# Six weight places, in-place low parts, late factors for two feed-forward norms, and grouped 512-column matmuls in a three-layer float32 forward pass

## The reference

```python
for l in range(2):                                   # first kind
    h = rmsnorm(x, g_mix[l]);  proj = h @ w_in[l]    # gates, convolution, three attentions
    branch = einsum('bsnc,ncd->bsnd', ys, w_branch[l])
    x = x + sum(sigmoid(gate) * branch) @ w_out[l]
    x = x + conv_ffn(rmsnorm(x, g_ffn[l]), w_up[l], ..., w_down[l])     # D_FF = 2816
h = rmsnorm(x, norm_mix_2);  ...                     # second kind: SSD, LRU, retention
x = x + merged @ w_o_2
x = x + conv_ffn_2(rmsnorm(x, norm_ffn_2), ...)      # FFN_DIM = 3072
out = rmsnorm(x, norm_final_2)

def rmsnorm(x, g): return x * rsqrt(mean(x * x, -1) + EPS) * g
def conv_ffn(h, w_up, conv_w, conv_b, w_down):
    gate, up = split(depthwise_conv(h @ w_up, conv_w, conv_b))
    return (silu(gate) * up) @ w_down
```

## Time and profile before

| | |
|---|---|
| three runs | 1458.43, 1458.99, 1459.16 us |
| profiled execution | 1458.09 us, of it 1456.3 us span of the core |
| TensorE busy | 1435.8 us, 99% of the span |
| GpSimd busy | 1183.8 us, 81% |
| ScalarE busy | 886.1 us, 61% |
| VectorE busy | 660.0 us, 45% |
| chain that ended last | 93% on TensorE, 2% VectorE, 2% ScalarE, 1% issue, 1% DMA |
| read from HBM | 249.56 MB, 172 GB/s over the span |

### The profile page before, as it was taken

The page is one execution under the profiler, slowest core; times in us unless marked ns, Lnnn a source line. Parts: engine busy times, 40 slices in busy tenths (PEclk is TensorE's granted clock), DMA queues, the critical chain, the costliest instruction groups (busy, mean ns, idle before and its releaser), DMA issues.

```text
span 1456.3 us, 29049 instructions
## 1 busy us (share of the span) xinstructions
PE 1435.8 (99%) x9420; PEld 1294.2 (89%) x9420; DVE 660.0 (45%) x1478; ACT 886.1 (61%) x1496; POOL 1183.8 (81%) x926
## 2 busy tenths in 40 slices
PE   8999999999999999999999999999999999999998
PEld 7899998888888899988888889999899999888887
DVE  3653444444445733355444456660563642433333
ACT  5665645766666655647666666866445544655554
POOL 5876686999879876787998979899576899789895
PEclk9999999999999999999999999999999999999999
DMA  7654454666556544454665666556444565566663
GB/s 246 201 159 146 145 160 144 199 193 187 188 178 202 167 153 143 150 178 144 198 190 189 184 212 199 161 176 188 130 145 125 152 189 185 157 190 186 190 188 101
DMA packets 80036, 251.80 MB, mean 173 GB/s; under 512 B 7632, under 2 KB 22480, under 8 KB 79440
## 3 DMA queue, kind: packets, MB, share of 16 engines
q1 hardware_dynamic: 79088, 245.72, 54.3%
q10 hardware_dynamic: 864, 4.92, 0.9%
HBM read 249.56 MB, written 1.05 MB: 172 GB/s over the span
## 4 chain that ended last, share of the span: by engine, by line
PE 93%; DVE 2%; ACT 2%; issue 1%; DMA 1%; POOL 0%; SPq 0%; DVEq 0%; ACTq 0%; POOLq 0%
PE psum L922 20%; PE psum L923 20%; PE psum L924 20%; PE psum L956 18%; PE psum L957 9%; PE psum L1033 1%; PE psum L1021 1%; DMA raw<-in_units 1%; PE psum L1052 1%; PE psum L1043 1%; DVE x L1463 1%; ACT w_hi L428 0%; PE psum L1316 0%; PE psum L1111 0%; PE psum L1352 0%
## 5 line engine op out<-in xcount | busy, mean ns | idle before, releaser
L403 POOL TENSOR_TENSOR w_lo<-raw,w_hi 128x512 fp32r<-128x512 f32 x461 | 602.8, 1308 | 257.2 <-ACT w_hi L428 247.6
L404 POOL TENSOR_TENSOR w_lo<-raw,w_hi 128x512 fp32r<-128x512 f32 x461 | 609.1, 1321 | 0.0
L428 ACT ACTIVATE w_hi<-raw 128x1024 fp32r<-128x1024 f32 x461 | 484.7, 1054 | 92.3 <-PE psum L924 76.6
L956 PE MATMUL psum<-both,w_hi 128*128 128x512 f32 x1088 | 387.6, 399 | 0.0
L922 PE MATMUL psum<-both,w_hi 128*128 128x256 f32 x1192 | 345.4, 290 | 2.3 <-POOL w_lo L404 2.3
L924 PE MATMUL psum<-both,w_hi 128*128 128x256 f32 x1192 | 336.9, 283 | 0.0
L923 PE MATMUL psum<-both,w_lo 128*128 128x256 f32 x1192 | 336.9, 283 | 0.0
L957 PE MATMUL psum<-both,w_lo 128*128 128x256 f32 x1088 | 305.3, 281 | 0.0
L956 PEld LDWEIGHTS psum<-both,w_hi 128*128 128x128 f32 x1088 | 204.3, 188 | 51.2 <-POOL w_lo L404 0.4
L922 PEld LDWEIGHTS psum<-both,w_hi 128*128 128x128 f32 x1192 | 228.0, 191 | 11.8 <-issue 8.6
L923 PEld LDWEIGHTS psum<-both,w_lo 128*128 128x128 f32 x1192 | 228.2, 191 | 0.3
(11 more groups left out here) (276 smaller groups left out, 2118.6 us busy)
## 6 DMA issues: line engine op xcount, KB each, us to landing
raw<-in_units SPq DMA_DIRECT2D x461, 512.0 KB, 3.6
arena<-in_consts ACTq DMA_DIRECT2D x1, 2320.0 KB, 9.4
arena<-in_bias ACTq DMA_DIRECT2D x2, 1024.0 KB, 5.0
arena<-in_consts SPq DMA_DIRECT2D x1, 1657.0 KB, 8.4
out<-arena SPq DMA_DIRECT2D x4, 256.0 KB, 2.6
pre<-in_x SPq DMA_DIRECT2D x2, 256.0 KB, 2.9
arena<-in_x SPq DMA_DIRECT2D x2, 256.0 KB, 4.7
prm<-in_params ACTq DMA_DIRECT2D x2, 153.5 KB, 3.4
```

What stands on the lines that cost most here:

```text
L403: pool.tensor_tensor(w_lo[s][:, 0:D // 2], raw[s][:, 0:D // 2], w_hi[s][:, 0:D // 2].bitcast(F32), ALU.subtract)
L404: pool.tensor_tensor(w_lo[s][:, D // 2:D], raw[s][:, D // 2:D], w_hi[s][:, D // 2:D].bitcast(F32), ALU.subtract)\
L428: act.activation(w_hi[s][:, :], raw[s][:, :], ACT.Copy).then_inc(hi_ready, d.inc(hi_ready))
L956: pe.matmul(bank(4 + k), blocks_of(w_hi[s], c), both[:, 2 * c * T:2 * (c + 1) * T], start=(c == 0), stop=False, skip_group_check=True)
```

## The change

It has these parts:

1. There are six places for weights. `w_lo[s]` lies in the same memory as `raw[s]`, so the low part is written over the raw weights. SyncE now waits for TensorE to be done with unit u-6 before it loads unit u. ScalarE's `high()` waits only for the landing, and GpSimd only for the high part. Six units are loaded at the start.
2. ScalarE makes one high part more ahead at the start (`norm(..., 4)` for 3). In the feed-forward norms two `high()` stand where one stood, and the one after the first two feed-forwards is gone.
3. The norms ahead of the three feed-forwards are late: `late_norm`. x is turned unscaled, by transposes, between the pieces of the last product (`last_two_turning`). h's parts are made of x times g. The factor of each token is made meanwhile, spread over the partitions by two small matmuls into bank 2, and copied to `rstd`. `add_low` multiplies each up unit's sum by it, one more VectorE instruction for each of the 136 up units.
4. The first two up units run together, chunk by chunk. Every other up unit has its eight 512-column matmuls first and then its eight of 256 columns.
5. Five loops of TensorE and ScalarE in the third layer are written out.

```diff
 RING = 4
+W_RING = 6
...
-        raw = [sb(f"raw{s}", D) for s in range(RING)]
-        w_hi = [sb(f"w_hi{s}", D, F32R) for s in range(RING)]
-        w_lo = [sb(f"w_lo{s}", D, F32R) for s in range(RING)]
+        raw = []
+        with ExitStack() as landing:
+            for s in range(W_RING):
+                raw.append(landing.enter_context(nc.sbuf_tensor(f"raw{s}", [P, D], F32)))
+        w_lo = [sb(f"w_lo{s}", D, F32R) for s in range(W_RING)]
+        w_hi = [sb(f"w_hi{s}", D, F32R) for s in range(W_RING)]
...
+            d.skip(unit_done, RING)
+            def landing_free(u):
+                if u is None or u >= W_RING:
+                    sp.wait_ge(unit_done, d.next(unit_done))
...
-            def load(index, s):
-                sp.wait_ge(hi_ready, d.next(hi_ready))
-                sp.wait_ge(lo_ready, d.next(lo_ready))
+            def load(index, s, u=None):
+                landing_free(u)
...
             def low(s):
-                pool.wait_ge(raw_full[s], d.next(raw_full[s]))
                 pool.wait_ge(hi_ready, d.next(hi_ready))
-                pool.wait_ge(unit_done, d.next(unit_done, 1, "slot"))
...
                     act.wait_ge(raw_full[s], d.next(raw_full[s]))
-                    act.wait_ge(unit_done, d.next(unit_done, 1, "slot"))
                     act.activation(w_hi[s][:, :], raw[s][:, :], ACT.Copy).then_inc(hi_ready, d.inc(hi_ready))
...
+            def late_norm(gain, spare):
+                act.activation(small[:, 57:58], small[:, 60:61], ACT.Sqrt)
+                act.wait_ge(x_ready, d.next(x_ready, 2))
+                act.activation(tok(arena, 2), tok(x, 0), ACT.Square, accum_out=small[:, 0:1])
+                act.wait_ge(x_ready, d.next(x_ready))
+                act.activation(tok(arena, 3, 0, 512), tok(x, 1, 0, 512), ACT.Square, accum_out=small[:, 1:2])\
+                    .then_inc(part_ready, d.inc(part_ready))
+                for c in range(CH):
+                    if c % 4 == 0:
+                        act.wait_ge(turned, d.next(turned))
+                    if c >= 2:
+                        act.wait_ge(hlo_ready, d.next(hlo_ready))
+                    act.activation(chunk(h_hi, c), raw_chunk(c, spare), ACT.Copy, scale=prm[:, gain + c:gain + c + 1])\
+                        .then_inc(hhi_ready, d.inc(hhi_ready))
+                    if c == 3:
+                        high()
+                ...
+                high()
+                act.wait_ge(factors, d.next(factors))
+                act.activation(rstd[:, :], bank(2, 0, T), ACT.Copy).then_inc(rows_ready, d.inc(rows_ready))
...
-                norm(load_params1, P1["g_mix"], 2 if layer else 3, True)
+                norm(load_params1, P1["g_mix"], 2 if layer else 4, True)
...
-                norm(lambda: None, P1["g_ffn"], 1)
+                late_norm(P1["g_ffn"], SPARE1)
...
                         feed_high(jj % 2, jj % 2 * 2 + 1)
-                high()
...
                 for c in range(CH):
-                    if first is not None:
-                        pe.wait_ge(first, d.next(first))
                     pe.matmul(bank(4 + k), blocks_of(w_hi[s], c), both[:, 2 * c * T:2 * (c + 1) * T], start=(c == 0), stop=False, skip_group_check=True)
+                for c in range(CH):
                     last = pe.matmul(slot(k), blocks_of(w_lo[s], c), chunk(h_hi, c), start=False, stop=(c == CH - 1), skip_group_check=True)
...
+            def last_two_turning(hi, lo, c, ready):
+                ...
+                for half, g in ((0, 0), (0, 1), (1, 0)):
+                    for k in range(2):
+                        ...
+                        last = piece(half, g, k)
+                    last.then_inc(acc_done, d.inc(acc_done))
+                pe.wait_ge(slot_free, d.value(slot_free, "wait", -RING))
+                pe.wait_ge(x_ready, d.next(x_ready, 2))
+                turn_raw(0, range(CH))
+                piece(1, 1, 0).then_inc(unit_done, d.inc(unit_done))
+                pe.wait_ge(x_ready, d.next(x_ready))
+                turn_raw(1, range(4)).then_inc(turned, d.inc(turned))
+                piece(1, 1, 1).then_inc(unit_done, d.inc(unit_done))
...
             def feed_forward(n):
-                up_unit(hlo_ready)
-                for _ in range(3):
+                pair = []
+                for _ in range(2):
+                    pair.append((unit(), next_slot()))
+                    pe.wait_ge(slot_free, d.next(slot_free))
+                for c in range(CH):
+                    pe.wait_ge(hlo_ready, d.next(hlo_ready))
+                    for s, k in pair:
+                        ...
+                    if c == 1:
+                        pe.wait_ge(x_ready, d.next(x_ready))
+                        turn_raw(1, range(4, CH)).then_inc(turned, d.inc(turned))
+                pe.wait_ge(root_rows, d.next(root_rows))
+                for half in range(2):
+                    last = pe.matmul(bank(2, half * P, P), small[:, 4 + half:5 + half].to_broadcast([P, P]), ident, start=True, stop=True)
+                last.then_inc(factors, d.inc(factors))
+                for _ in range(2):
                     up_unit()
...
-                last_two(y_hi, y_lo, 2 * CH - 2, flo_ready)
-                turn_norm()
+                last_two_turning(y_hi, y_lo, 2 * CH - 2, flo_ready)
...
                 dve.wait_ge(low_out, d.next(low_out))
-                dve.tensor_tensor(slot(k), slot(k), low_part(k)[1], ALU.add).then_inc(sum_ready, d.inc(sum_ready))
+                dve.tensor_tensor(slot(k), slot(k), low_part(k)[1], ALU.add).then_inc(vec, d.inc(vec))
+                dve.wait_ge(d.last, d.made(d.last))
+                dve.tensor_tensor(slot(k), slot(k), rstd[:, :], ALU.mult).then_inc(sum_ready, d.inc(sum_ready))
...
+            def late_norm(gain, spare):
+                ...
+                for q in range(3):
+                    dve.wait_ge(acc_done, d.next(acc_done))
+                    add(q)
+                dve.wait_ge(part_ready, d.next(part_ready))
+                dve.tensor_scalar(small[:, 3:4], small[:, 1:2], 1.0 / D, EPS, ALU.mult, ALU.add).then_inc(rest_ready, d.inc(rest_ready))
+                h_low(0)
+                dve.wait_ge(unit_done, d.next(unit_done))
+                add(3)
+                for c in range(1, CH):
+                    h_low(c)
+                d.skip(turned, 2)
+                dve.wait_ge(sd_ready, d.next(sd_ready))
+                dve.reciprocal(small[:, 4:6], small[:, 6:8]).then_inc(root_rows, d.inc(root_rows))
+                dve.wait_ge(rows_ready, d.next(rows_ready))
```

144 lines of the change are left out of this document (83 added, 61 removed).

## The result

The changed kernel took 1479.03 us (median of 4 runs, 1476.20 to 1482.27), the kernel before on the same chip 1459.08 us (1458.43 to 1459.23). The ratio is 1.0138, with a 95% interval of 1.0126 to 1.015: slower by 20 us. The forecast was 1463.2 us, with a range that ended at 1467.5.

What follows compares the result with a forecast made beforehand. TensorE, busy 1435.8 of 1456.3 us at full clock, was taken as the bound. 2 x 2.1 + 2 x 2.1 + 0.8 + 0.5 - 5.5 = +4.2 us gave 1462.3, as a median 1463.2; range 1455.3 to 1467.5.

Steps and rivals of the forecast that it cites:

- At the start: Start of the program: six early loads and wider prefetch change nothing TensorE waits for; 0, within 0.5 us either way.
- The boundary: Step from the last product into the feed-forward: the fifth up unit starts 2.1 us later in each of the first two.
- the third boundary: Same step into the third feed-forward: one scaled copy, then the Gelu waits for two taps; unit 393 0.8 us later.
- The ends: Ends of the feed-forwards: late copy and multiply add 2.1 us in each of the first two, 0.5 in the third.
- The grouping: Up units' matmuls ordered by size, 118 units counted: 5.5 us saved.
- The rival that it gives nothing: Up units: the order of sizes may not cause the slow pace, so no saving; +9.7 us, 1468.7; chance 12%.
- The steady loop: Feed-forward loops: ScalarE is held back but with room; the 136 multiplies, 58 us, lie in VectorE's idle time.
- the fourth rival: GpSimd becomes the bound because each multiply holds it up: 1470 to 1480 us; chance 4%.
- The third rival: Attention and third layer: `high()` waits for fresh landings, making ScalarE late; +3 us more, 1466; chance 12%.
- The first: Boundaries and ends: weights land before ScalarE comes to the `high()`, leaving only the multiply; 3.5 us less, 1455.5; chance 20%.

Runs made afterwards that it cites:

- e2: The changed kernel, with SyncE issuing units 4 and 5 and the table of constants only when the first norm's parameters have landed: 1475.67 us, ratio 1.011.
- e9: The changed kernel, with only the table of constants held back until the first parameters have landed: 1474.09 us, ratio 1.0107.
- e5: The changed kernel plus 15 useless 512-column matmuls behind the fourth up unit of each feed-forward, filling TensorE's wait: 1469.32 us, ratio 1.0067.
- e3: The changed kernel, with both copies of low sums ahead of the high part at the first tile of the first two feed-forwards: 1469.41 us, ratio 1.0072.
- e4: The changed kernel, with ScalarE one high part less ahead through the feed-forwards: 1461.83 us, ratio 1.0022.
- e8: The changed kernel with e2's edit, first-tile copies ahead of the high part in all feed-forwards, and one high part less ahead in the first two: 1452.46 us.
- e6: The changed kernel without the multiply of each up unit's sum by the token's factor: 1475.49 us, ratio 1.0112.
- e1: The kernel before with only the matmuls grouped by size, in up units outside the first of each feed-forward: 1453.55 us, ratio 0.9963.
- e7: The changed kernel with the feed-forward norms of before, no multiply, ScalarE's old order around them, and e2's edit: 1454.79 us, ratio 0.9971.
- e10: The kernel of e8 run again, beside e11 on one chip: 1452.48 us, ratio 0.9954.
- e11: The kernel before with the grouped matmuls alone, run again beside e10 on one chip: 1454.43 us, ratio 0.9967.

## Why the prediction was wrong

The side was right, the size was not: +4.2 us forecast, +18 in the trace and +20 in the median. Two things were priced at nothing and one term was too small.

**The failed steps.** *"At the start ... the six early loads and the wider prefetch change nothing that TensorE waits for: 0, within 0.5 either way."* It was +4.54 us, 3.88 of it from the late parameters. I weighed what the loads do to GpSimd's pace and not what else was in flight. The parameters' DMA at 10.6 us was in the trace of before, with 3.2 us to landing, and the order of SyncE's queue was in the diff. e2 shows the cause, e9 that it was the table and not the two units. The other 0.66, at unit 4, came from a late high part.

*The price of a wait.* Each wait that I added was priced at its length. The earlier trace rows show a full clock in every slice, and I took that as given instead of as something that TensorE's steady work keeps up. The waits that I forecast myself, near 4 us at unit 72 and near 2.7 at the ends, let it fall at three of the four places where the wait was about 3.5 us, 7.2 us in all. e5 shows this by filling the wait, e3 by taking it away. With both mistakes off (4.5 + 7.2 = 11.7) the trace would be 6.4 us longer than before, against 4.2.

**The boundary** was right in mechanism and size. Without the clock the steps are 3.46 - 1.57 = 1.9 and 4.66 - 2.84 = 1.8 us against 2.1; the wait was 3.57 for 3.9, and the third boundary +0.86 for +0.8. e3 and e4 show both parts of it, the high part between the copies and the landing.

**The ends** had the right mechanism; the term was too small: 2.9, and 5.85 - 2.81 = 3.0, for 2.1. I had the copy late by 1.8 and it was late by 2.5: unit 129 ended at 426.67 and the weights that take its place were there at 430.99, 4.3 us later, where I had counted 3.7. Why this landing took longer than the median is open. The multiply's share, 0.47 in e4 and e8, was as worked out (0.5) where no landing is in the way.

**The grouping** gave 1.59 + 1.60 + 1.74 = 4.9 us for 5.5, and 5.3 alone. The rival that it gives nothing is out. The Trainium skill's page "TensorE: Matmul & The Clock Gate" (LDWEIGHTS, step by step) says only that the next weights load while a matmul runs; what fails for this stream is the step from there to "the order of the sizes doesn't matter".

**The steady loop** was right: ScalarE waits for landings everywhere, and TensorE for nothing. Nearly all of the 136 multiplies are hidden. GpSimd's halves take 1306 and 1316 ns in the changed kernel, 1308 and 1316 without the multiply (e6) and 1308 and 1321 before, so neither the multiplies nor the six places slow it, which was the fourth rival. The third rival, late high parts in the attentions, was worth 0.4 us and not 3, with 0.66 more at unit 4. The first, loads in time, failed on the landing: ScalarE came to unit 74's `high()` 1.31 us ahead of it.

## What to carry to other kernels

Price a wait of a busy TensorE at its length, and one of some 2 us or more at 1.5 to 2.8 us on top in case the clock falls; a single stop may cost more than a hundred hidden instructions. When loads are brought forward, list every other transfer that is issued after them and ask who waits for it first. A ring with more places moves the wait from "the place is free" to "the transfer has landed"; look for the one instruction behind such a wait that others need, and put it ahead.

## What the runs showed of the hardware that was not expected

- The clock's fall is not certain. Over the thirteen traces, behind the first 12 us, among TensorE's waits of 2 us and more, it did not fall behind 2.15 (e4), six times 2.27 or 2.28 (the kernel before, e1, e7, e8, e10, e11), 2.69 (e9), 2.73 (e3), 2.76 (changed kernel), 3.30 and 3.40 (e6), 3.47 (changed kernel) and 3.53 us (e2). It fell behind 2.12 (e9), 2.15 (e4), 2.27 (e2), 2.65 and 2.67 (e5), 2.80 (e2), 2.81 twice (e6), 3.32 (e6), 3.47 (e9), 3.49 (changed kernel) and behind all fifteen of 3.54 to 4.81 us. Once it fell behind 1.25 us, at unit 4 of e4. Behind the waits of the feed-forwards a fall cost 1.5 to 2.8 us of slower matmuls.
- Such falls go with a spread of the runs: 6 us over four runs of the changed kernel, 8 over ten of e4, 1.4 over four of e8. They are not all of it, since e3, with falls in its trace, has 0.7 over four, and e7, with none, 3.9 over nine.
- Grouping matmuls by size is worth 0.04 us in eight couples of 512 and 256 columns, on the same instructions. What it is that costs between unlike neighbours stays open.
